# Block two's first projection: a buffer for each modulation condition, the feed-forward gate's columns moved to the mixer's output projection, one request per chunk

## The chip, the cores and the metric

The kernel runs on one core of a Trainium2 chip. The metric is the time of one execution on the device in microseconds (us). Three runs of the kernel before took 3015.27, 3014.43 and 3009.39 us, with a median of 3014.43 us. One more execution was recorded by the profiler; it took 3022.09 us, and every row below is from it.

## The reference, cut to what matters

Two transformer blocks run in sequence on 512 latent tokens of 1024 features; the second block also carries 256 context tokens. Each layer is steered by six rows of 1024 numbers (shift, scale and gate of the mixer, shift, scale and gate of the feed-forward), which come from a matrix product with a condition vector. In the second block there are two conditions, one for the latent tokens and one for the context tokens, and both see the same weights:

```python
mod = (silu_c @ ada_w[i] + ada_b[i])[:, None, :]
mod_c = (silu_cc @ ada_w[i] + ada_b[i])[None, None, :]
sh_m, sc_m, g_m, sh_f, sc_f, g_f = jnp.split(mod, 6, axis=-1)
h = modulate(rmsnorm(x, norm_mix_w[i]), sh_m, sc_m)
hc = modulate(rmsnorm(ctx, norm_mix_w[i]), shc_m, scc_m)
y, y_c = ab_mixer(h, hc, ...)              # first projection, mixing, output projection
x = x + g_m * y
x = x + g_f * swiglu(modulate(rmsnorm(x, norm_ffn_w[i]), sh_f, sc_f), w_gate, w_up, w_down)
```

The matrix `ada_w` of one layer has 1024 x 6144 numbers. The gate of the feed-forward, `g_f`, is the last of the six rows to be used: it is needed only after `w_down`.

## The kernel before, in words

Every large product is done in stages. A stage streams its weights in chunks of 128 output columns: SP loads a chunk into one of two raw buffers (`weights_raw`), ScalarE (ACT) rounds it to the high part (line L360), GpSimd (POOL) subtracts to get the low part (L406), and TensorE (PE) multiplies: two of three groups of products need the high part alone (L246, L247), the third needs the low part (L251). SP may reload a raw buffer when POOL has made the low part of what was in it. ACT, or VectorE (DVE), takes the result out of PSUM. The first two chunks of a stage that also norms or splits its input are done in another loop (L455, L456, L461), and their low parts are made by DVE (L412).

The modulation rows are computed on DVE beside such stages, as *rides*. A ride is one load of `n` blocks of 128 columns of `ada_w` into one of two buffers, then for every block and condition one multiply-and-sum of 128 x 1024 numbers (L1338), then an addition of the bias (L1343), which counts up the semaphore `added`. Ahead of the rides the conditions are loaded by SP (L1305, spread to all 128 partitions), ACT takes their sigmoid into PSUM (L1319) and DVE multiplies (L1326). A ride's load is issued by POOL (L1309 for the first two, L1313 for the others) and waits until the ride that used that buffer before has been added.

Layer 0 of block two begins with such a stage, `Project`: 12 chunks over 512 + 256 tokens, with 16 rides of two blocks, which give four of the six rows (mixer gate, feed-forward shift, scale and gate). Its instructions stand in the order that the code issues them, on each engine:
- SP: norm weights, bias, condition 0, condition 1, then the weight chunks from the third on. There is one buffer for a condition, so the load of condition 1 waits for DVE's product of condition 0, and the weight loads stand behind it.
- ACT: two high parts, 16 shifts of the norm (L1516), the sigmoids, then in turn copies out of PSUM (L2790) and high parts.
- POOL: two rides' loads, low part of chunks 2 and 3 (counted from 0); from chunk 4 to chunk 9 after each low part two loads of rides; the low parts of chunks 10 and 11 without a load; then two loads.
- DVE: norm, conditions, 16 rides, and one addition of 1 (L1351).

The next stage, `Values` (4 chunks, L2999, L3000, L3008), shares weights buffers and PSUM with it; its first product waits until `added` is at the number of rides. After the mixing itself comes the stage `GemmResidual` with the mixer's output projection: 8 chunks over all 768 tokens. There DVE splits the input (L510), makes two low parts (L412), and after each chunk adds the gated result to the residual stream (L1857); ACT squares (L1411) and POOL sums the squares (L1418) for the next norm. Other stages of this class carry rides already, between the residual additions; here there is none. The last row, `g_f`, is read first in the feed-forward's down projection, which follows.

Of the kernel before, what the change touches and what calls it, by code (L numbers as in the profile page):

```python
# [25 lines left out]
P = 128  # L26
D = 1024
KD = D // P
# [4 lines left out]
DEPTH = 2  # L33
# [1245 lines left out]
class Modulation:  # L1279
# [3 lines left out]
    def __init__(self, nc, M, ctx, s, w, b, cond, first, n, conds=2, out=None, room=None, bank=2):  # L1283
        self.nc, self.M, self.s, self.w, self.first, self.n = nc, M, s, w, first, n
        self.b, self.cond, self.conds, self.bank = b, cond, conds, bank
        self.out = M.mod_next if out is None else out
        if room:
            self.W, self.J = room
        else:
            self.W = ctx.enter_context(nc.sbuf_tensor(f"{M.blocks}_mod_w", [P, 2, n, D], F32))  # L1290
            self.J = ctx.enter_context(nc.sbuf_tensor(f"{M.blocks}_mod_c", [P, D], F32))
        self.B = ctx.enter_context(nc.sbuf_tensor(f"{M.blocks}_mod_b", [P, 2 * N_MOD], F32))
        self.acc = ctx.enter_context(nc.sbuf_tensor(f"{M.blocks}_mod_acc", [P, 2, 2 * n], F32))
        self.ready = (s["r0"], s["r1"])

    def silu_cond(self, c):
        return self.M.PS[:, self.bank + 4 * c:self.bank + 2 + 4 * c, :].rearrange("p a b -> p (a b)")

    def load(self, sp):
        s = self.s  # L1300
        sp.dma_start(self.B[:], self.b).then_inc(s["bias_in"], 16)
        for c in range(self.conds):
            if c:
                sp.wait_ge(s["summed"], c)
            sp.dma_start(self.J[:], self.cond[c].partition_broadcast(P)).then_inc(s["cond_in"], 16)  # L1305

    def load_first(self, eng):
        for u in range(2):
# [5 lines left out]

    def sigmoid(self, act):
        for c in range(self.conds):
            act.wait_ge(self.s["cond_in"], 16 * (c + 1))
            for j in range(2):
                self.nc.scalar.activation(self.M.PS[:, self.bank + 4 * c + j, :], self.J[:, j * 512:(j + 1) * 512],  # L1319
                                          ACT.Sigmoid).then_inc(self.s["sig"], 1)  # L1320

    def conditions(self, dve):
        self.nc.vector.memset(self.acc[:], 0.0).then_inc(self.s["bias_in"], 16)
        for c in range(self.conds):
            dve.wait_ge(self.s["sig"], 2 * c + 2)
            self.nc.vector.tensor_tensor(self.silu_cond(c), self.J[:], self.silu_cond(c),  # L1326
                                         ALU.mult).then_inc(self.s["summed"], 1)
        dve.wait_ge(self.s["summed"], self.conds)
        dve.wait_ge(self.s["bias_in"], 32)
# [1353 lines left out]
class Project:  # L2683
# [34 lines left out]
    def gpsimd(self, pool):  # L2718
        R, S = self.R, self.S
        if R:  # L2720
            R.load_first(pool)

            def two(pool, i, u):
                for v in range(2):
                    R.load_next(pool, 2 * i + (u - 1), v)

            pairs = (self.rides // 2 - 1) // 2
            S.lows(pool, two, pairs + 1, 1, not self.H)
            for n in range(2 * pairs + 1, self.rides // 2):
                for v in range(2):  # L2730
                    R.load_next(pool, n, v)
        else:
            S.lows(pool, first=not self.H)

# [756 lines left out]
def block_two(nc, M, A):  # L3491
# [5 lines left out]
    def tensor(ctx, name, shape, dt=F32):  # L3497
        return ctx.enter_context(M.nc.sbuf_tensor("two_" + name, shape, dt))

    with ExitStack() as ctx:  # L3500
        B = Buffers()
        B.PT, B.V = tensor(ctx, "ab_projT", [P, 12, TA]), tensor(ctx, "ab_values", [P, TA // P, 1024])
        with ExitStack() as inner:
            M.hR = tensor(inner, "ab_h_parts", [P, 2, KD, TA], F32R)
            rms_stats(nc, M, TA)
            room = (tensor(inner, "ab_mod_w", [P, 2, 2, D]), B.V[:, 2])
            ride = (modulation(A, DEPTH, 2), A["b_ada"][DEPTH], A["cond"][1], 2 * KD, 2, 2 * KD, room)
            first = Project(nc, M, inner, proj_weights(A, DEPTH), 12, B.PT, [(0, T), (T, TC)], None, ride=ride,
                            parts=(4,), KP_most=2 * KD,
                            norm=(A["norm_mix"][0], both, 0, 1, B.V[:, 0:2].rearrange("p t (u v) -> p (t u) v", v=T)))  # L3510
            run_stages(nc, [first, Values(nc, M, inner, ab_v, 1024 // VC, B.V, TA // P, ab_out, first)])
        B.mixT = tensor(ctx, "ab_mixT", [P, KD, TA])
        with ExitStack() as inner:
            B.rel = tensor(inner, "rel", [P, 8, 16 * 64])
            spatial_gate(nc, M, A, B)
            attend2(nc, M, B)
        M.hR = tensor(ctx, "ab_mix_parts", [P, 2, KD, TA], F32R)
        gemm_residual(nc, M, ab_out, M.hR, both, 2, ffn_up(A, 0, 0), mix=B.mixT, stats=True)
    feed_forward(nc, M, A, 0, both, (8, 8, 6), cd_k)

    adopt(nc, M, (1, 4))
# [249 lines left out]
```

## Time and profile before

| | |
|---|---|
| median of three runs | 3014.43 us (3009.39 to 3015.27) |
| profiled execution | 3022.09 us, of which 3020.4 us lie between its first and its last instruction |
| TensorE busy | 2652.4 us, 88% of the span; mean granted clock 0.935 |
| VectorE, ScalarE, GpSimd busy | 1465.4, 1022.3 and 788.4 us |
| first projection of block two, norm included | from 1367.9 to 1504.8 us |
| `Values` after it | from 1504.8 to 1576.9 us |
| mixer's output projection | from 1713.0 to 1795.3 us |

TensorE is busy for most of each of the three stages in the table, so the place to read is where it waits in them. A busy share of 88% says little about them. "Idle before" in a row of the timeline, in square brackets, is how long the engine had waited before that instruction, and for whom.

### The profile page before, as it was taken

What the parts mean: (1) busy time and instruction counts of PE and PEld (TensorE: products, weight loads), DVE (VectorE), ACT (ScalarE), POOL (GpSimd) and SP (SyncE); (2) the same over time, 40 slices, a digit from 0 to 9 for tenths busy, and PEclk for the clock granted to TensorE, in tenths of its full rate; (3) what the DMA queues carried; (4) which work ended last, traced back from release to release, by engine and by line L of the source; (5) the groups of instructions that cost most, each with busy time, mean ns of one, the idle gap of its engine ahead of it and who ended that gap; (6) DMA issues with size and microseconds to landing.
All of it is one profiled execution on the core that took longest, in us unless ns stands there. A gap on an engine that the chain in (4) does not pass through costs nothing. (4 is left out here: it accounts for less than half of the span.)

```text
span 3020.4 us, 41597 instructions
## 1 busy us (share of the span) xinstructions
PE 2652.4 (88%) x14918; PEld 1974.8 (65%) x14918; DVE 1465.4 (49%) x2887; ACT 1022.3 (34%) x1617; POOL 788.4 (26%) x401
## 2 busy tenths in 40 slices
PE   2998879977998869967787889999999799799997
PEld 2786453335784633326685678888888687688886
DVE  7677661335786642346706634472424575231122
ACT  3656431116566232123225632112122342322122
POOL 0451031102450311101310032232333331234443
PEclk9999889988998979988898989999999899899999
DMA  7530158953620259833611012241433311222322
GB/s 252 208 119 34 36 212 327 358 180 108 214 84 20 99 226 366 312 110 126 222 47 46 15 56 84 91 146 63 140 112 114 117 56 43 70 97 94 101 88 79
DMA packets 100697, 398.19 MB, mean 132 GB/s; under 512 B 17432, under 2 KB 27064, under 8 KB 80320
## 3 DMA queue, kind: packets, MB, share of 16 engines
q1 hardware_dynamic: 71472, 303.38, 28.7%
q0 software_dynamic: 28928, 92.30, 8.1%
q8 instruction: 90, 1.47, 0.2%
q14 instruction: 63, 0.52, 0.1%
q10 hardware_dynamic: 144, 0.52, 0.0%
HBM read 490.00 MB, written 23.59 MB: 170 GB/s over the span
## 5 line engine op out<-in xcount | busy, mean ns | idle before, releaser
L406 POOL TENSOR_TENSOR 17_w_part<-weights_raw,17_w_part 128x2048 fp32r<-128x2048 f32 (+2 forms) x44 | 146.4, 3329 | 397.2 <-ACT 17_w_part L360 397.2
L2600 DVE TENSOR_TENSOR ffn_silu<-ffn_silu,PS 128x512 f32<-128x512 f32 x66 | 37.5, 596 | 416.8 <-ACT ffn_silu L2582 416.8
L2346 PE MATMUL PS<-one_weights_more,10_h_tokens 128*64 128x512 f32 (+1 forms) x1024 | 231.2, 604 | 2.5 <-DVE 10_h_tokens L2456 2.5
L246 PE MATMUL PS<-ffn_h_parts,17_w_part 128*128 128x512 f32 (+1 forms) x640 | 202.6, 337 | 2.4 <-DVE xT L1857 1.5
L406 POOL TENSOR_TENSOR 29_w_part<-weights_raw,29_w_part 128x2048 fp32r<-128x2048 f32 (+2 forms) x36 | 147.8, 4105 | 215.1 <-ACT 29_w_part L360 215.1
L247 PE MATMUL PS<-ffn_h_parts,17_w_part 128*128 128x512 f32 (+1 forms) x640 | 201.6, 337 | 0.0
L406 POOL TENSOR_TENSOR 3_w_part<-weights_raw,3_w_part 128x1024 fp32r<-128x1024 f32 (+1 forms) x52 | 142.9, 2749 | 205.1 <-ACT 3_w_part L360 205.1
L1857 DVE SCALAR_TENSOR_TENSOR xT<-PS,mod,xT 128x512 f32 x104 | 66.3, 664 | 234.3 <-PE PS L251 201.3
L2582 ACT ACTIVATE ffn_silu<-PS 128x512 f32<-128x512 f32 x66 | 32.4, 526 | 405.7 <-PE PS L251 378.4
L2346 PEld LDWEIGHTS PS<-one_weights_more,10_h_tokens 128*64 128x64 f32 x1024 | 78.3, 139 | 133.3 <-issue 127.2
L246 PE MATMUL PS<-one_mix_parts,3_w_part 128*128 128x512 f32 x352 | 140.8, 400 | 15.2 <-ACT 3_w_part L360 15.2
L247 PE MATMUL PS<-one_mix_parts,3_w_part 128*128 128x512 f32 x352 | 139.7, 397 | 0.0
L246 PEld LDWEIGHTS PS<-ffn_h_parts,17_w_part 128*128 128x128 f32 x640 | 121.3, 190 | 15.6 <-issue 1.7
L247 PEld LDWEIGHTS PS<-ffn_h_parts,17_w_part 128*128 128x128 f32 x640 | 121.7, 190 | 13.0
L2464 DVE SCALAR_TENSOR_TENSOR 10_hid<-10_silu,one_slot_gate,PS 128x256 f32<-128x256 f32 x32 | 15.4, 480 | 233.8 <-ACT 10_silu L2427 233.8
L246 PE MATMUL PS<-ffn_h_parts,29_w_part 128*128 128x512 f32 x320 | 124.6, 389 | 0.0
L247 PE MATMUL PS<-ffn_h_parts,29_w_part 128*128 128x512 f32 x320 | 124.5, 389 | 0.0
L2369 PE MATMUL PS<-one_weights_more,10_hid_turned 128*64 128x512 f32 (+1 forms) x512 | 117.0, 598 | 2.5 <-ACT 10_hid_turned L2420 2.5
L251 PE MATMUL PS<-ffn_h_parts,17_w_part 128*128 128x512 f32 (+1 forms) x640 | 115.0, 337 | 0.0
L246 PE MATMUL PS<-ffn_hidden,17_w_part 128*128 128x512 f32 (+1 forms) x346 | 111.0, 340 | 2.6 <-ACT 17_w_part L360 2.6
L247 PE MATMUL PS<-ffn_hidden,17_w_part 128*128 128x512 f32 (+1 forms) x346 | 110.0, 340 | 0.0
L251 PEld LDWEIGHTS PS<-ffn_h_parts,17_w_part 128*128 128x128 f32 x640 | 99.8, 190 | 13.4
(666 smaller groups left out, 6591.5 us busy)
## 6 DMA issues: line engine op xcount, KB each, us to landing
one_weights_more<-in_w_gu SPq DMA_DIRECT2D x128, 1024.0 KB, 9.5
one_weights_more<-in_w_down SPq DMA_DIRECT2D x64, 1024.0 KB, 8.6
weights_raw<-in_f_gu SPq DMA_DIRECT2D x44, 1024.0 KB, 4.9
weights_raw<-in_w_proj SPq DMA_DIRECT2D x60, 512.0 KB, 3.6
one_values<-in_w_ada POOLq DMA_DIRECT2D x24, 1024.0 KB, 6.9
ffn_shared<-in_w_ada POOLq DMA_DIRECT2D x24, 1024.0 KB, 7.0
weights_raw<-in_w_ada SPq DMA_DIRECT2D x32, 512.0 KB, 9.5
two_ab_mod_w<-in_w_ada POOLq DMA_DIRECT2D x16, 1024.0 KB, 5.4
```

Of the source, the lines that this page charges most:

```text
L246: nc.tensor.matmul(out, w[0], x[1], start=(j == 0), stop=False)
L247: nc.tensor.matmul(out, w[0], x[0], start=False, stop=False)
L251: mm = nc.tensor.matmul(out, w[1], x[0], start=False, stop=(last and j == len(pairs) - 1))
L406: self.nc.gpsimd.tensor_tensor(self.part[:, u, 1], self.raw[:, u], self.part[:, u, 0].bitcast(F32), ALU.subtract).then_inc(self.count["spl ...
L1857: nc.vector.scalar_tensor_tensor(out=x, in0=M.PS[:, 4 * u + a:4 * u + a + 1, 0:nt], scalar=g, in1=x, op0=ALU.mult, op1=ALU.add).then_inc(s ...
L2346: mm = nc.tensor.matmul(M.PS[rows(h), 2 + i % 2, :], h_[:, i % 2, k, rows(h)], weights(i, h, k * 2 * FE), start=(k == 0), stop=(k == KD - 1))
L2369: mm = nc.tensor.matmul(M.PS[rows(h), 5 + part, :], hidT[:, i % 2, f, rows(h)], weights(i, h, 2 * SLOT + f * D + part * 512), start=(f == ...
L2464: nc.vector.scalar_tensor_tensor(out=hid[:, i % 2, :], in0=sl[:], scalar=D_.gate[:, u:u + 1], in1=M.PS[:, 2 + i % 2, FE:2 * FE], op0=ALU.mult,
L2582: ins = nc.scalar.activation(sl[:, u, off:off + nt], M.PS[:, 4 * u + a, 0:nt], ACT.Silu)
L2600: ins = nc.vector.tensor_tensor(sl[:, u, off:off + nt], sl[:, u, off:off + nt], M.PS[:, 4 * u + 2 + a, 0:nt], ALU.mult)
```

## The change

The diff, whole but for the header:

```diff
--- before.py
+++ after.py
@@ -1284,8 +1284,10 @@
         self.nc, self.M, self.s, self.w, self.first, self.n = nc, M, s, w, first, n
         self.b, self.cond, self.conds, self.bank = b, cond, conds, bank
         self.out = M.mod_next if out is None else out
+        self.J2 = None
         if room:
-            self.W, self.J = room
+            self.W, self.J = room[0:2]
+            self.J2 = room[2] if len(room) > 2 else None
         else:
             self.W = ctx.enter_context(nc.sbuf_tensor(f"{M.blocks}_mod_w", [P, 2, n, D], F32))
             self.J = ctx.enter_context(nc.sbuf_tensor(f"{M.blocks}_mod_c", [P, D], F32))
@@ -1296,13 +1298,16 @@
     def silu_cond(self, c):
         return self.M.PS[:, self.bank + 4 * c:self.bank + 2 + 4 * c, :].rearrange("p a b -> p (a b)")
 
+    def condition(self, c):
+        return self.J2[:] if c and self.J2 is not None else self.J[:]
+
     def load(self, sp):
         s = self.s
         sp.dma_start(self.B[:], self.b).then_inc(s["bias_in"], 16)
         for c in range(self.conds):
-            if c:
+            if c and self.J2 is None:
                 sp.wait_ge(s["summed"], c)
-            sp.dma_start(self.J[:], self.cond[c].partition_broadcast(P)).then_inc(s["cond_in"], 16)
+            sp.dma_start(self.condition(c), self.cond[c].partition_broadcast(P)).then_inc(s["cond_in"], 16)
 
     def load_first(self, eng):
         for u in range(2):
@@ -1314,16 +1319,17 @@
 
     def sigmoid(self, act):
         for c in range(self.conds):
-            act.wait_ge(self.s["cond_in"], 16 * (c + 1))
+            act.wait_ge(self.s["cond_in"], 16 * (self.conds if self.J2 is not None else c + 1))
             for j in range(2):
-                self.nc.scalar.activation(self.M.PS[:, self.bank + 4 * c + j, :], self.J[:, j * 512:(j + 1) * 512],
+                self.nc.scalar.activation(self.M.PS[:, self.bank + 4 * c + j, :],
+                                          self.condition(c)[:, j * 512:(j + 1) * 512],
                                           ACT.Sigmoid).then_inc(self.s["sig"], 1)
 
     def conditions(self, dve):
         self.nc.vector.memset(self.acc[:], 0.0).then_inc(self.s["bias_in"], 16)
         for c in range(self.conds):
             dve.wait_ge(self.s["sig"], 2 * c + 2)
-            self.nc.vector.tensor_tensor(self.silu_cond(c), self.J[:], self.silu_cond(c),
+            self.nc.vector.tensor_tensor(self.silu_cond(c), self.condition(c), self.silu_cond(c),
                                          ALU.mult).then_inc(self.s["summed"], 1)
         dve.wait_ge(self.s["summed"], self.conds)
         dve.wait_ge(self.s["bias_in"], 32)
@@ -2720,15 +2726,7 @@
         if R:
             R.load_first(pool)
 
-            def two(pool, i, u):
-                for v in range(2):
-                    R.load_next(pool, 2 * i + (u - 1), v)
-
-            pairs = (self.rides // 2 - 1) // 2
-            S.lows(pool, two, pairs + 1, 1, not self.H)
-            for n in range(2 * pairs + 1, self.rides // 2):
-                for v in range(2):
-                    R.load_next(pool, n, v)
+            S.lows(pool, R.load_next, self.rides // 2, 0, not self.H)
         else:
             S.lows(pool, first=not self.H)
 
@@ -3503,8 +3501,8 @@
         with ExitStack() as inner:
             M.hR = tensor(inner, "ab_h_parts", [P, 2, KD, TA], F32R)
             rms_stats(nc, M, TA)
-            room = (tensor(inner, "ab_mod_w", [P, 2, 2, D]), B.V[:, 2])
-            ride = (modulation(A, DEPTH, 2), A["b_ada"][DEPTH], A["cond"][1], 2 * KD, 2, 2 * KD, room)
+            room = (tensor(inner, "ab_mod_w", [P, 2, 2, D]), B.V[:, 2], B.V[:, 3])
+            ride = (modulation(A, DEPTH, 2), A["b_ada"][DEPTH], A["cond"][1], 2 * KD, 2, 3 * KD // 2, room)
             first = Project(nc, M, inner, proj_weights(A, DEPTH), 12, B.PT, [(0, T), (T, TC)], None, ride=ride,
                             parts=(4,), KP_most=2 * KD,
                             norm=(A["norm_mix"][0], both, 0, 1, B.V[:, 0:2].rearrange("p t (u v) -> p (t u) v", v=T)))
@@ -3515,7 +3513,9 @@
             spatial_gate(nc, M, A, B)
             attend2(nc, M, B)
         M.hR = tensor(ctx, "ab_mix_parts", [P, 2, KD, TA], F32R)
-        gemm_residual(nc, M, ab_out, M.hR, both, 2, ffn_up(A, 0, 0), mix=B.mixT, stats=True)
+        room = (B.V[:, 0:2].rearrange("p (u n) d -> p u n d", n=1), B.V[:, 2], B.V[:, 3])
+        gemm_residual(nc, M, ab_out, M.hR, both, 2, ffn_up(A, 0, 0), mix=B.mixT, stats=True,
+                      ride=(modulation(A, DEPTH, 1), A["b_ada"][DEPTH], A["cond"][1], 5 * KD, 1, 2, M.mod, room))
     feed_forward(nc, M, A, 0, both, (8, 8, 6), cd_k)
 
     adopt(nc, M, (1, 4))
```

The first projection has 12 rides instead of 16 (mixer gate, feed-forward shift and scale). The four others, `g_f`, become 8 rides of one block in the mixer's output projection, with their own loads of the bias and of both conditions; the buffers are pieces of the values tensor, `B.V`, which is free in both places. Each condition has a buffer of its own in both stages, ACT waits for both, and SP no longer waits for DVE between them. In the first projection POOL issues one ride's load after each low part, from the third chunk to the last.

SP at the start of the first projection, before. Semaphores show the name of their first use: `b3_conv_in` is here the count of DVE's products, `b3_summed` the count of low parts made.

```order
L1477 DMA 12_norm_w<-in_norm_mix 128x8
L1301 DMA 12_mod_b<-in_b_ada 128x96
L1305 DMA two_ab_values<-in_cond 128x1024
L1305 DMA two_ab_values<-in_cond 128x1024 [waits b3_conv_in]
L345 UNCONDITIONAL_BRANCH
L345 ISA
L349 ISA [waits b3_summed]
L349 DMA weights_raw<-in_w_proj 128x1024
```

And now:

```order
L1483 DMA 12_norm_w<-in_norm_mix 128x8
L1306 DMA 12_mod_b<-in_b_ada 128x96
L1310 DMA two_ab_values<-in_cond 128x1024 x2
L345 UNCONDITIONAL_BRANCH
L345 ISA
L349 ISA [waits b3_summed]
L349 DMA weights_raw<-in_w_proj 128x1024
```

The load of condition 1 no longer waits, and the weight loads behind it wait for low parts alone.

POOL in the first projection, before, in the loop over chunks 4 to 9 (`b3_sig` is the count of high parts, `b4_used` is `added`):

```order
L406 TENSOR_TENSOR 12_w_part<-weights_raw,12_w_part 128x1024 [waits b3_sig]
L1312 ISA
L1313 ISA [waits b4_used]
L1313 DMA two_ab_mod_w<-in_w_ada 128x2x1024
L1313 ISA [waits b4_used]
L1313 DMA two_ab_mod_w<-in_w_ada 128x2x1024
L332 REGISTER_ALU
L406 TENSOR_TENSOR 12_w_part<-weights_raw,12_w_part 128x1024 [waits b3_sig]
```

And now, in the loop over chunks 2 to 11:

```order
L406 TENSOR_TENSOR 12_w_part<-weights_raw,12_w_part 128x1024 [waits b3_sig]
L1317 REGISTER_ALU
L1318 ISA [waits b4_used]
L1318 DMA two_ab_mod_w<-in_w_ada 128x2x1024
L332 REGISTER_ALU
L406 TENSOR_TENSOR 12_w_part<-weights_raw,12_w_part 128x1024 [waits b3_sig]
```

Two loads with their waits stood between a low part and the next; now it is one.

DVE in the mixer's output projection, before, from the split of the input to the first residual addition (`b3_cond_in` is the count of finished chunks):

```order
L510 TENSOR_TENSOR two_ab_mix_parts<-two_ab_mixT,two_ab_mix_parts 128x768 [waits b3_added] x8
L412 TENSOR_TENSOR 16_w_part<-weights_raw,16_w_part 128x1024 [waits b3_sig] x2
L1849 UNCONDITIONAL_BRANCH
L1849 ISA
L1857 ISA [waits b3_cond_in]
L1857 REGISTER_ALU
L1857 SCALAR_TENSOR_TENSOR xT<-PS,mod,xT 128x512
L1857 ISA
L1857 SCALAR_TENSOR_TENSOR xT<-PS,mod,xT 128x256
```

And now, from the two low parts to the bias of the first ride; the residual addition, L1863, comes behind it (`b3_affine` is the count of sigmoids, `b3_taken` the landing of a ride's load):

```order
L412 TENSOR_TENSOR 16_w_part<-weights_raw,16_w_part 128x1024 [waits b3_sig] x2
L1329 MEMSET 16_mod_acc 128x4
L1332 TENSOR_TENSOR PS<-two_ab_values,PS 128x1024 [waits b3_affine] x2
L1855 UNCONDITIONAL_BRANCH [waits b3_iw_done,b3_conv_in]
L1855 ISA
L1344 ISA two_ab_values,16_mod_acc<-two_ab_values,PS 128x1024 [waits b3_taken]
L1344 ISA 16_mod_acc 128x1
L1347 ISA
L1344 ISA two_ab_values,16_mod_acc<-two_ab_values,PS 128x1024 [waits b3_conv_in]
L1344 ISA 16_mod_acc 128x1
L1347 REGISTER_ALU
L1349 ISA [waits b3_conv_in]
```

The conditions' products and a ride of two sums now stand ahead of each residual addition.

## Rows read from the trace of the kernel before

**Rows 1.** Windows: window, length, busy time (count) by engine, granted clock, DMA, GB/s.
```profile
core 0: us, PE busy (x) PEld busy (x) DVE busy (x) ACT busy (x) POOL busy (x), PEclk, DMA share, GB/s
1401.00:1405.00 4.00, 3.69 (x9) 2.92 (x10) 3.83 (x8) 2.08 (x4) 3.65 (x2) 0.50 0.03 10
1412.00:1454.00 42.00, 42.00 (x242) 37.10 (x241) 27.90 (x50) 9.88 (x16) 14.71 (x11) 1.00 0.59 201
1505.00:1510.00 5.00, 5.00 (x24) 5.00 (x25) 0.00 (x0) 1.67 (x1) 3.26 (x1) 0.50 0.01 3
```
**Rows 2.** Timeline of TensorE: start, duration, engine, line, operation, [idle before <- releaser].
```profile
1401.32 0.79 PE L246 MATMUL PS<-two_ab_h_parts,12_w_part 128*128 128x512 f32 x1 [8.04 <-ACT 12_w_part L360]
1411.53 0.40 PE L246 MATMUL PS<-two_ab_h_parts,12_w_part 128*128 128x512 f32 x1
...
1444.97 0.40 PE L246 MATMUL PS<-two_ab_h_parts,12_w_part 128*128 128x512 f32 x1
...
1471.85 4.23 PE L251 MATMUL PS<-two_ab_h_parts,12_w_part 128*128 128x512 f32 x16 [2.79 <-POOL 12_w_part L406]
1475.88 0.63 PE L246 MATMUL PS<-two_ab_h_parts,12_w_part 128*128 128x512 f32 x1
...
1504.84 0.56 PE L2999 MATMUL PS<-12_w_part,two_ab_h_parts 128*128 128x256 f32 x1 [10.12 <-DVE mod L1351]
```
**Rows 3.** Waits in projection and `Values`: who waited for whom: total us, times, longest.
```profile
POOL two_ab_mod_w L1313 <- DVE mod L1343: 43.6, 12, 4.7
...
PE PS L251 <- POOL 12_w_part L406: 5.4, 3, 2.8
```
**Rows 4.** Timeline of SP's queue in the first projection.
```profile
1392.92 0.33 SPq L1305 DMA_DIRECT2D two_ab_values<-in_cond  x1
1393.64 78.75 SPq L349 DMA_DIRECT2D weights_raw<-in_w_proj  x10
```
**Rows 5.** Timeline of ScalarE in the first projection.
```profile
1389.22 1.28 ACT L1319 ACT_TABLE_LOAD   x1
...
1397.27 1.12 ACT L1319 ACTIVATE PS<-two_ab_values 128x512 f32<-128x512 f32 x2 [5.64 <-DMA two_ab_values<-in_cond]
1398.33 0.85 ACT L2790 ACTIVATE two_ab_projT<-PS 128x512 f32<-128x512 f32 x2
1400.21 1.06 ACT L360 ACTIVATE 12_w_part<-weights_raw 128x1024 fp32r<-128x1024 f32 x1 [1.03 <-DMA weights_raw<-in_w_proj]
...
1477.39 1.06 ACT L360 ACTIVATE 12_w_part<-weights_raw 128x1024 fp32r<-128x1024 f32 x1 [0.31 <-ACT two_ab_projT L2790]
```
**Rows 6.** Timeline of GpSimd in the first projection.
```profile
1468.69 0.72 POOL L1313 DMA_DIRECT2D two_ab_mod_w<-in_w_ada  x1 [4.54 <-DVE mod L1343]
1469.43 2.37 POOL L406 TENSOR_TENSOR 12_w_part<-weights_raw,12_w_part 128x1024 fp32r<-128x1024 f32 x1
...
1485.93 0.74 POOL L1313 DMA_DIRECT2D two_ab_mod_w<-in_w_ada  x1 [0.33 <-DVE mod L1343]
```
**Rows 7.** Timeline of VectorE at the end of the first projection.
```profile
1493.96 1.22 DVE L1338 CUSTOM_DVE_ANT_0 two_ab_values<-two_ab_mod_w,PS 128x1024 f32<-128x1024 f32 x1 [3.05 <-DMA two_ab_mod_w<-in_w_ada]
...
1499.24 1.22 DVE L1338 CUSTOM_DVE_ANT_0 two_ab_values<-two_ab_mod_w,PS 128x1024 f32<-128x1024 f32 x1
...
1504.43 0.16 DVE L1343 TENSOR_TENSOR mod<-12_mod_acc,12_mod_b 128x4 f32 x1 [0.18 <-DVE 12_mod_acc L1338]
```
**Rows 8.** Tile `two_ab_mod_w` (1 MB a load): issue to landing of its loads.
```profile
DMA to landing us min/median/max: 5.2/5.4/9.4
```
**Rows 9.** Timeline of VectorE in the mixer's output projection.
```profile
1722.77 2.35 DVE L412 TENSOR_TENSOR 16_w_part<-weights_raw,16_w_part 128x1024 fp32r<-128x1024 f32 x2
1735.77 2.19 DVE L1857 SCALAR_TENSOR_TENSOR xT<-PS,mod,xT 128x512 f32 x4 [10.65 <-PE PS L461]
...
1787.65 1.14 DVE L1857 SCALAR_TENSOR_TENSOR xT<-PS,mod,xT 128x512 f32 x2 [7.23 <-PE PS L251]
```
**Rows 10.** Tile `7_mod_w`, block one's rides of one block (0.5 MB): issue to landing.
```profile
DMA to landing us min/median/max: 3.5/5.0/6.3
```

## The prediction, made before the changed kernel had run

> **What bounds the kernel now.** I read the timeline of TensorE first, for its gaps, then the queues of the engines it waited for, then the windows for the clock. In steady state the first projection of block two is bound by TensorE: chunk 3 starts at 1411.53 and chunk 7 at 1444.97, four chunks in 33.44 us, 8.36 us each, with TensorE busy for all of the 42.00 us of that window at full clock, 2.4 GHz [rows 1, 2]. Everything else in the stage is a wait of TensorE, and there are three kinds.
>
> The first is the gap of 8.04 us before chunk 2 [rows 2]. The releaser named is ACT's high part, but that one waited for weights [rows 5], and SP's queue shows why: the load of condition 1 left at 1392.92, and the first of ten weight loads behind it at 1393.64 [rows 4]. The second is the three waits for a low part, 5.4 us together [rows 3]: the longest, 2.79 us at 1471.85 [rows 2], ends with a low part that POOL could begin at 1469.43 only, because it had waited 4.54 us for DVE to free a ride's buffer [rows 6]. POOL waited so 12 times, 43.6 us in all [rows 3]. The third is the gap of 10.12 us before `Values` [rows 2], until DVE has finished the last ride [rows 7]. DVE is not late by its own work alone: the last but one ride waited 3.05 us for a load [rows 7] that POOL had issued behind two low parts [rows 6].
>
> After each long gap the granted clock is 0.50, the level of 1.2 GHz: in 1401 to 1405 and in 1505 to 1510 [rows 1].
>
> **The change part by part.** All sums go against the profiled execution, 3022.09 us (span 3020.4).
>
> *A buffer for each condition.* SP's weight loads are no longer behind DVE's product. They wait for low parts that DVE makes during the first pair of chunks, so they land well before that pair ends at 1393.28 (1401.32 less 8.04). Both conditions land early too: the one issued at 1392.92 let ACT start at 1397.27, 4.35 us later [rows 4, 5], and ACT first asks for them at 1389.22. From there ACT needs 1.28 for the table and twice 1.12 for four sigmoids [rows 5], to 1392.7, so it is free when the pair ends. Then come a copy (0.85), a hand-over of about 0.31, and the high part (1.06) [rows 5]: chunk 2 starts 2.2 us after the pair, at 1395.5. The gap goes from 8.04 to 2.2: **5.8 us**. Chunk 2 itself took 10.21 us (1401.32 to 1411.53) against 8.36, as its first part ran at the lower clock; if the short gap keeps the clock, that is **1.85 us**. For the shorter gap the bounds are the waits in this stage: behind the one of 2.79 us, 16 products took 4.23 us and the next matmul 0.63 us, where the same kind takes 0.40 in the steady state [rows 2]; so it may not be kept, and I hold 0 to 1.85, taking 1.85 because 2.2 is below 2.79.
>
> *One request per chunk, 12 rides.* Chunks 3 to 11 took from 1411.53 to 1494.72 (1504.84 less 10.12), 83.19 us; nine chunks of 8.36 are 75.24. The excess, **7.95 us**, is the three waits and what the clock lost behind them. Would a low part still be late? POOL's order is now low part, wait, load. Rides begin about 1394.4, behind the sigmoids and DVE's two products, and take 5.35 us each (1499.24 to 1504.59, [rows 7]); the load after low part n needs ride n-2 to be done. That holds POOL only for the first two or three chunks, until about 1411, when low parts have over 5 us before TensorE asks for them (high products take two thirds of 8.36). Later a chunk of 8.36 is longer than a ride of 5.35, so POOL does not wait. I take all 7.95, with 5 as the low bound.
>
> *The end of the rides.* With chunk 2 at 1395.5, chunk 10 starts at 1462.4 and chunk 11 ends at 1479.1. The last load follows low part 11. ACT makes high part 11 at 1.51 us into chunk 10 (1477.39 against 1475.88, [rows 2, 5]), done at 2.6; the low part of 2.37 [rows 6] is done at 5.0. The load lands 5.2 to 9.4 us later, median 5.4 [rows 8], and the one that shared the DMA engines with the weights of `Values` took 8.0 (1485.93 to 1493.96, [rows 6, 7]). That sharing is there again, since SP's load waits for the same low part. With 5.4 the last ride ends 15.8 us after chunk 10's start, with 8.0 it ends at 18.4; chunk 11 ends at 16.7. So TensorE waits 0 to 1.9 us (0.25 from DVE's end to its start included); I take 1.0. The gap of 10.12 becomes 1.0: **9.1 us**. The Trainium skill (DMA: Bandwidth & Descriptors, Anatomy of one DMA — SWDGE (gpsimd) path) puts such a transfer at 2.0 us plus its bytes over 436 GB/s, which would be, as an estimate, 4.4 us and no wait at all, a gain of 28.2 in place of 27.2 below. The trace does not agree: its shortest is 5.2.
>
> *The start of `Values`.* The five microseconds from 1505 ran at half the clock [rows 1]; without the long gap that returns half of them, **2.5 us**.
>
> *The rides in the mixer's output projection.* What moves there: on SP a bias and two conditions ahead of the weight loads, which start over 10 us later; on POOL two loads at the start and six between low parts and sums, at most 0.74 each [rows 6]; on ACT a table load and four sigmoids (3.5 us) behind the split, inside a wait that lasts to the end of the first pair; on DVE two products (1.23 each, as an estimate the same as a sum's 1.22) and 8 rides of two sums, 2.8 us each (half of 5.35 and the bias). DVE stands idle 10.65 us before the first residual addition and 7.23 before the last [rows 9]: 2.5 + 2.8 fit in the first, 2.8 in the second. A ride stands ahead of a residual addition, so a late load would hold it. A low part ends about 3.7 us into a chunk (1.06 and 2.37 with hand-overs), and the load is out at 4.5; it lands 3.5 to 6.3 us later [rows 10], the ride takes 2.8, and the residual addition is due at the end of the chunk's successor but one. There is room for a landing of 17 us, except in the last chunk, where the addition is on the path to the norm: there the limit is 9.4 us (load out 4.5 us into the chunk that starts two times 8.36 before the residual addition at 1787.65 [rows 9], so at 1775.4). **0 us**, between -0.5 and 3.
>
> Sum: 5.8 + 1.85 + 7.95 + 9.1 + 2.5 = 27.2 us, so 2994.9 us for an execution like the profiled one. That one stood 7.7 us above the median of the runs, 3014.43, from which I take the 27.2: **2987 us**.
>
> **The rivals.**
> 1. The rides still set the end. If the last load takes the longest landing, 9.4 us [rows 8], the last ride ends 19.8 us after chunk 10's start and the gap is 3.3, long enough for the lower clock, as the one of 2.79 shows. The gain loses 2.3 and 2.5: 22.4 us, 2992 us. For it speaks that two 1 MB transfers go out together; against it that the worst comparable one took 8.0.
> 2. The change does not do what it says: the gap before chunk 2 stays, because the weights or the second condition land late for another reason. It gives back 5.8 + 1.85: gain 19.6, 2995 us. Against it: 21 us lie between the stage's start at 1367.9 and the first use of a condition at 1389.22 [rows 5].
> 3. The work is moved, not hidden. If nothing of DVE's work in the output projection were covered, it would cost 8 x 2.8 + 2.5, some 25 us, and the kernel would stay within 0.2% (3012 us). Against it are the idle times in [rows 9].
> 4. Slower than before: loads of the rides in the output projection land late, DVE holds the residual additions, and PSUM banks come free late. It costs TensorE time from a landing of 17 us on, twice over the eight chunks, and the norm from 9.4 us on; to eat 27.2 us all of them need about 24 us, and then 3018 us or more. The longest in [rows 10] is 6.3.
>
> **How the numbers follow.** My forecast has 0.80, rival 1 0.07, rival 2 0.04, rival 3 0.05, rival 4 0.04. The forecast's own range is a gain of 20 to 30 us (the clock in the short gap, 3 us of waits left, 1.9 at the end, 3 in the output projection; above, no wait at the end and the rest of a colder start); with the spread of the runs, 3009 to 3015, I give 2978 to 3001 us, which holds rivals 1 and 2. A measurement of this kernel can tell about 0.2%, 6 us, from no change. Faster by more than that: forecast, rivals 1 and 2, 0.91; within it: rival 3, 0.05; slower: rival 4, 0.04.
>
> **What would show it.** In the new profile SP's second condition leaves right behind the first and the weights follow before 1390; TensorE's gap before chunk 2 is 2 to 3 us, chunk 2 takes 8.4; no wait for a low part above 0.5 us; the gap before `Values` is under 2 us, and the stage with the norm lasts some 112 us instead of 137. The output projection keeps its 82 us. I am wrong if DVE or POOL appears as TensorE's releaser in the output projection, or if the gap before `Values` is 4 us or more.

## The result, and the profile after

The changed kernel took 2985.02 us (median of four runs, 2981.76 to 2988.96), the kernel before 3014.85 us (four runs, 3009.39 to 3017.19). The ratio is 0.9903 with a 95% interval of 0.9890 to 0.9917: 29.8 us less, the interval is 25 to 33. The forecast was 2987 us, a gain of 27.2 in a range of 20 to 30.

The two profiled executions, 3022.09 and 2985.17 us, lie 36.9 us apart, more than the medians. The stages show where. From the first product of the projection to the first product of the feed-forward, all that the change touches, before took 429.4 us and after 400.2: 29.2 us. Another 6.6 us lie ahead of it, in code that did not change: the first product comes at 1372.4 in the profile of before and at 1365.8 after, and over the profiles of all the kernels below between 1361.2 and 1372.4. The remaining 1.1 us lie behind. So the profiled execution of before was a late one, and all that follows is measured from the first product of the projection on.

TensorE in the changed kernel, at the starts of chunk 2 and of `Values` (start, duration, engine, line, operation, idle before and releaser):

```profile
1388.14 0.50 PE L246 MATMUL PS<-two_ab_h_parts,12_w_part 128*128 128x512 f32 x1 [1.51 <-ACT 12_w_part L360]
1388.48 0.39 PE L247 MATMUL PS<-two_ab_h_parts,12_w_part 128*128 128x512 f32 x1
...
1455.14 0.40 PE L246 MATMUL PS<-two_ab_h_parts,12_w_part 128*128 128x512 f32 x1
...
1473.34 0.36 PE L2997 MATMUL PS<-12_w_part,two_ab_h_parts 128*128 128x256 f32 x1 [1.32 <-DVE mod L1357]
1473.54 0.28 PE L2998 MATMUL PS<-12_w_part,two_ab_h_parts 128*128 128x256 f32 x1
```

These answer to [rows 2]. The gap of 8.04 us is one of 1.51, the gap of 10.12 one of 1.32, and the first products behind them take 0.50 and 0.36 us, where those of before took 0.79 and 0.56; the second ones take 0.39 and 0.28, as in the steady state. Chunk 2 starts at 1388.14 and chunk 10 at 1455.14: eight chunks in 67.00 us, 8.375 each, all at the pace of the steady state. The windows behind the two gaps show the clock (window, length, busy time by engine, granted clock, DMA share, GB/s):

```profile
1388.00:1392.00 4.00, 3.86 (x17) 3.19 (x18) 3.90 (x7) 1.91 (x4) 2.41 (x1) 1.00 0.11 10
1473.00:1478.00 5.00, 4.66 (x39) 4.69 (x40) 0.26 (x2) 1.91 (x1) 2.75 (x1) 1.00 0.49 197
```

1.00, the level of 2.4 GHz, in both; [rows 1] had 0.50. Who waited for whom from 1365 to 1560:

```profile
POOL two_ab_mod_w L1318 <- DVE mod L1349: 8.9, 4, 3.2
...
PE PS L246 <- ACT 12_w_part L360: 1.5, 1, 1.5
...
PE PS L2997 <- DVE mod L1357: 1.3, 1, 1.3
```

TensorE's waits for a low part are gone from the list, and POOL's for a ride's buffer went from 43.6 us in 12 times [rows 3] to 8.9 in four. The queues show the two causes. SP, then ACT ahead of chunk 2:

```profile
1362.36 0.90 SPq L1310 DMA_DIRECT2D two_ab_values<-in_cond  x2
1375.98 68.33 SPq L349 DMA_DIRECT2D weights_raw<-in_w_proj  x10
```
```profile
1382.62 1.28 ACT L1324 ACT_TABLE_LOAD   x1
1383.92 2.16 ACT L1324 ACTIVATE PS<-two_ab_values 128x512 f32<-128x512 f32 x4
1386.01 0.85 ACT L2788 ACTIVATE two_ab_projT<-PS 128x512 f32<-128x512 f32 x2
1387.03 1.06 ACT L360 ACTIVATE 12_w_part<-weights_raw 128x1024 fp32r<-128x1024 f32 x1 [0.17 <-ACT two_ab_projT L2788]
```

Both conditions leave together, the weights 13.6 us later, 11 us before ACT asks for them; the four sigmoids run without a break, where those of the second condition had stood 5.64 us [rows 5]. And the end of the rides, on POOL and on DVE:

```profile
1457.77 2.39 POOL L406 TENSOR_TENSOR 12_w_part<-weights_raw,12_w_part 128x1024 fp32r<-128x1024 f32 x1 [5.33 <-ACT 12_w_part L360]
1460.11 0.74 POOL L1318 DMA_DIRECT2D two_ab_mod_w<-in_w_ada  x1
```
```profile
1467.72 1.22 DVE L1344 CUSTOM_DVE_ANT_0 two_ab_values<-two_ab_mod_w,PS 128x1024 f32<-128x1024 f32 x1 [2.60 <-DMA two_ab_mod_w<-in_w_ada]
...
1472.92 0.16 DVE L1349 TENSOR_TENSOR mod<-12_mod_acc,12_mod_b 128x4 f32 x1 [0.18 <-DVE 12_mod_acc L1344]
1473.13 0.17 DVE L1357 TENSOR_SCALAR mod<-mod 128x16 f32<-128x16 f32 x1
```

The last load goes out at 1460.11 and lands 7.6 us later, when the sum starts; the last ride ends 17.9 us after chunk 10's start. All twelve loads of this tile, issue to landing, and then the seven that leave from 1410.96 on:

```profile
DMA to landing us min/median/max: 5.3/6.7/10.8
```
```profile
DMA to landing us min/median/max: 6.3/6.8/8.3
```

The median is later than before [rows 8]. Each of the seven leaves within 0.5 us of a load of weights. The three ahead of them leave 1.8 us or more behind one and land after 5.3 to 5.5 us; the first two, which leave beside the two conditions, after 8.8 and 10.8.

### The profile page after: what moved, and what is told of

It is laid out like the page before. It is cut to its first block and busy times, and to the rows that moved or that the text cites. A ratio compares the mean times of both kernels' runs of the same rounds, so it can differ in the third digit from the quotient of the medians.

```text
span 2983.5 us, 41616 instructions
## 1 busy us (share of the span) xinstructions
PE 2640.4 (88%) x14918; PEld 1964.7 (66%) x14918; DVE 1480.1 (50%) x2894; ACT 1025.2 (34%) x1622; POOL 790.8 (27%) x405
## 5 line engine op out<-in xcount | busy, mean ns | idle before, releaser
L1863 DVE SCALAR_TENSOR_TENSOR xT<-PS,mod,xT 128x512 f32 x104 | 66.4, 664 | 196.7 <-PE PS L251 169.3
L246 PEld LDWEIGHTS PS<-ffn_h_parts,17_w_part 128*128 128x128 f32 x640 | 121.3, 190 | 15.6 <-issue 1.7
L247 PEld LDWEIGHTS PS<-ffn_h_parts,17_w_part 128*128 128x128 f32 x640 | 121.5, 190 | 13.1
L2375 PE MATMUL PS<-one_weights_more,10_hid_turned 128*64 128x512 f32 (+1 forms) x512 | 117.0, 598 | 2.6 <-ACT 10_hid_turned L2426 2.6
L360 ACT ACTIVATE 17_w_part<-weights_raw 128x2048 fp32r<-128x2048 f32 (+2 forms) x46 | 65.7, 1432 | 125.3 <-PE PS L251 117.7
```

Source lines behind the costliest of these rows:

```text
L246: nc.tensor.matmul(out, w[0], x[1], start=(j == 0), stop=False)
L247: nc.tensor.matmul(out, w[0], x[0], start=False, stop=False)
L360: self.nc.scalar.activation(self.part[:, u, 0], self.raw[:, u], ACT.Copy).then_inc(self.count["high_done"], 1)
L1863: nc.vector.scalar_tensor_tensor(out=x, in0=M.PS[:, 4 * u + a:4 * u + a + 1, 0:nt], scalar=g, in1=x, op0=ALU.mult, op1=ALU.add).then_inc(s ...
L2375: mm = nc.tensor.matmul(M.PS[rows(h), 5 + part, :], hidT[:, i % 2, f, rows(h)], weights(i, h, 2 * SLOT + f * D + part * 512), start=(f == ...
```

## The experiments

Diffs are against the changed kernel and cut to the lines that matter, with `...` for arguments left out; the comments that begin with # are mine. A first set takes the change apart. Three edits undo one part each:

```diff
# the old order: two requests per low part from the second pair on, the rest at the end
-            S.lows(pool, R.load_next, self.rides // 2, 0, not self.H)
+            def two(pool, i, u):
+                for v in range(2):
+                    R.load_next(pool, 2 * i + (u - 1), v)
+            pairs = (self.rides // 2 - 1) // 2
+            S.lows(pool, two, pairs + 1, 1, not self.H)
+            for n in range(2 * pairs + 1, self.rides // 2):
+                for v in range(2):
+                    R.load_next(pool, n, v)
# one buffer for the conditions
-            room = (tensor(inner, "ab_mod_w", [P, 2, 2, D]), B.V[:, 2], B.V[:, 3])
+            room = (tensor(inner, "ab_mod_w", [P, 2, 2, D]), B.V[:, 2])
# all 16 rides in the projection, none in the output projection
-            ride = (..., 2 * KD, 2, 3 * KD // 2, room)
+            ride = (..., 2 * KD, 2, 2 * KD, room)
-        gemm_residual(nc, M, ab_out, M.hR, both, 2, ffn_up(A, 0, 0), mix=B.mixT, stats=True, ride=(...))
+        gemm_residual(nc, M, ab_out, M.hR, both, 2, ffn_up(A, 0, 0), mix=B.mixT, stats=True)
```

The table has the total with its ratio to before, and from the profiles the stretches: from the first product to chunk 2 (A), chunk 2 to the start of the projection's last product (B), from there to the first product of `Values` (C: the gap and that product's own 0.28 us), from there to the start of the last product of `Values` (D), and the whole from the first product of the projection to the first of the feed-forward (E), in us.

| kernel | total (runs), us | ratio, 95% interval | A | B | C | D | E |
|---|---|---|---|---|---|---|---|
| before | 3014.85 (4) | | 28.9 | 93.1 | 10.4 | 71.7 | 429.4 |
| buffers alone | 3009.37 (12) | 0.9988 (0.9974 to 1.0003) | 22.4 | 91.1 | 10.3 | 71.1 | 420.3 |
| columns moved alone | 3004.01 (6) | 0.9962 (0.9949 to 0.9974) | 27.9 | 87.4 | 7.1 | 70.5 | 417.4 |
| moved and buffers | 2996.43 (5) | 0.9939 (0.9926 to 0.9952) | 22.4 | 85.0 | 6.9 | 71.1 | 410.7 |
| moved and order | 2995.68 (6) | 0.9936 (0.9924 to 0.9948) | 27.8 | 86.1 | 1.6 | 69.1 | 407.2 |
| the whole change | 2985.02 (4) | 0.9903 (0.9890 to 0.9917) | 22.4 | 83.6 | 1.6 | 69.1 | 400.2 |

The four parts were compared with 17 runs of before on their chip, 3013.19 us in the median. E is from one profile each.

**Buffers alone** (old order, 16 rides, none moved).

> The buffers alone: two condition buffers, but 16 rides in the first projection, the old order of requests on GpSimd, and no rides in the output projection. My theory: the gap before chunk 2 falls from 8.04 to about 1.5 us and chunk 2 runs at full clock (8.4 us instead of 10.2), while the three waits for low parts (5.4 us) and the gap before Values (10.1 us) stay, since rides and chunks move up together: gain 7 to 9 us. Rival (the conditions' order does not matter, the whole gain is that of the rides): gain under 2 us, gap still 8 us.

The gap before chunk 2 goes, the late low parts and the gap before `Values` stay. TensorE's waits, 1360 to 1520, and the start of `Values` with the clock behind it:

```profile
PE PS L3005 <- DVE mod L1357: 10.1, 1, 10.1
...
PE PS L251 <- POOL 12_w_part L406: 5.3, 3, 2.7
PE PS L246 <- ACT 12_w_part L360: 1.5, 1, 1.5
```
```profile
1487.91 0.55 PE L3005 MATMUL PS<-12_w_part,two_ab_h_parts 128*128 128x256 f32 x1 [10.07 <-DVE mod L1357]
```
```profile
1485.00:1492.00 7.00, 4.09 (x19) 4.12 (x20) 2.59 (x6) 1.91 (x1) 2.21 (x1) 0.50 0.01 2
```

In its stages it gains 9.1 us; the totals show 3.8 (3013.19 less 3009.37), and the interval reaches from a gain of 7.8 to a loss of 0.9. That difference stays open: the runs of this kernel scatter from 3000.50 to 3013.88 us, those of before on that chip from 3001.47 to 3019.96.

**Columns moved alone** (12 rides, old order, one buffer).

> The gate's columns moved alone: 12 rides in the first projection, 8 small ones in the output projection, but one condition buffer in the first projection and GpSimd's old order. My theory: the gap of 8.0 us before chunk 2 stays, the waits for low parts go (about 8 us with what the clock lost), and the gap before Values stays at some 6 to 8 us, because the last two loads are issued one behind the other after the last low part: gain 9 to 13 us. Rival (four rides fewer are enough for the end): gap before Values under 2 us, gain 18 to 20 us.

```profile
PE PS L246 <- ACT 12_w_part L360: 7.0, 1, 7.0
PE PS L3005 <- DVE mod L1357: 6.8, 1, 6.8
...
PE PS L251 <- POOL 12_w_part L406: 1.0, 1, 1.0
```

Four rides fewer take two of the three waits for a low part with them, but of the gap before `Values` only 3.3 us. The last two loads stand behind all low parts on POOL, so DVE is idle for 16.2 us until the first of them has landed, and then has two rides to do where the whole change has one. E falls by 12.0 us.

**Moved and buffers** (all but the new order).

> The whole change without the new order: two condition buffers, 12 rides, but GpSimd issues two requests per chunk from chunk 4 to 7 and the last two behind all low parts. My theory: gap before chunk 2 about 1.5 us, no waits for low parts, gap before Values 6 to 8 us with the lower clock behind it, so 7 to 10 us slower than the changed kernel, gain 17 to 22 us. Rival (the order is worth nothing, the number of rides decides): gap before Values under 2 us, gain as with the whole change, 27 to 30 us.

```profile
PE PS L3005 <- DVE mod L1357: 6.7, 1, 6.7
...
PE PS L251 <- POOL 12_w_part L406: 1.1, 1, 1.1
```

A falls to 22.4 as with the buffers alone, C stays at 6.9. One late low part is left, where I had expected none. What the order is worth is the difference to the whole change: 10.5 us of E, of which 5.3 in C, 2.1 in D and 1.4 in B; the rest lies behind `Values`. The totals show a gain of 16.8 us (3013.19 less 2996.43), a little under the 17 to 22 that I had expected.

**Moved and order** (all but the second buffer).

> The whole change without the second condition buffer in the first projection. My theory: the gap of 8.0 us and the slow chunk 2 are back, all else as in the changed kernel, with a gap before Values of 1 to 2 us: 7 to 9 us slower than the changed kernel, gain 19 to 22 us. Rival (with only 12 rides the late start of the weights is made up for later): within 2 us of the changed kernel.

```profile
PE PS L246 <- ACT 12_w_part L360: 6.9, 1, 6.9
...
PE PS L2997 <- DVE mod L1357: 1.3, 1, 1.3
```

No wait for a low part is left and C is 1.6, while the gap before chunk 2 stays at 6.9. The buffer is thus worth 7.1 us of E on top of the rest: 5.4 in A and 2.5 in B, where chunk 2 starts at the lower clock, less 0.9 elsewhere. In the totals this kernel gains 17.5 us, under the 19 to 22 that I had expected, while its E falls by 22.2; its profiled execution, 2987.50 us, was its fastest. The gap before chunk 2 comes from the single buffer alone. For the gap before `Values` fewer rides are not enough without the order; the order with all 16 rides was not tried.

A second set asks about the parts that the forecast had put at nothing or at a bound.

**No rides in the output projection.** The gate's columns are computed nowhere, so this kernel leaves out part of the computation:

```diff
-        gemm_residual(nc, M, ab_out, M.hR, both, 2, ffn_up(A, 0, 0), mix=B.mixT, stats=True, ride=(...))
+        gemm_residual(nc, M, ab_out, M.hR, both, 2, ffn_up(A, 0, 0), mix=B.mixT, stats=True)
```

> The changed kernel with the 8 rides of the output projection left out, so the columns of the feed-forward gate are not computed at all. My theory (they lie wholly beside TensorE's work): from the first product of the output projection to the first of the feed-forward 84 us as with them (84.2), total within 2 us of the changed kernel's. Rival (the moved rides cost something there): that stretch shorter by 1 us or more.

2990.88 us against 3017.13 of before (17 runs, as for the rest of this set), ratio 0.9916 (0.9903 to 0.9930): no faster than the whole change. The median is 5.9 us above that of the whole change, where I had expected 2; the intervals of the ratios overlap, and E is 400.6 us against 400.2. From the first product of the output projection to the first of the feed-forward it takes 84.1 us, the whole change 84.2, before 84.9. No cost of the rides there shows: 0.2 us is the difference of two single executions.

**Last loads ahead of the low parts.**

```diff
-            S.lows(pool, R.load_next, self.rides // 2, 0, not self.H)
+            S.wait(pool, "split_done", 2)
+            with pool.Fori(1, S.pairs - 1) as i:
+                for u in range(2):
+                    S.low(pool, 2 * i + u, u)
+                    R.load_next(pool, i, u)
+            for u in range(2):
+                R.load_next(pool, S.pairs - 1, u)
+                S.low(pool, 2 * S.pairs - 2 + u, u)
```

> The changed kernel, but for the last two chunks of the first projection GpSimd issues the ride's load ahead of the low part. My theory (what is left of the gap before Values, 1.3 us, is the landing of the last load, issued behind the last low part): that gap falls to about 0.2 us, no wait for a low part above 0.5 us, the stretch from the first projection to the feed-forward 1 us shorter; in the total within the noise. Rival (the last load is late because it shares the DMA engines with the weights of Values): gap still over 1 us.

POOL, then DVE, at the end of the projection:

```profile
1458.14 0.74 POOL L1318 DMA_DIRECT2D two_ab_mod_w<-in_w_ada  x1 [4.05 <-DVE mod L1349]
1460.11 2.40 POOL L406 TENSOR_TENSOR 12_w_part<-weights_raw,12_w_part 128x1024 fp32r<-128x1024 f32 x1 [1.23 <-ACT 12_w_part L360]
```
```profile
1468.80 0.18 DVE L1357 TENSOR_SCALAR mod<-mod 128x16 f32<-128x16 f32 x1
```

And TensorE's last low products of chunk 11:

```profile
1471.41 2.84 PE L251 MATMUL PS<-two_ab_h_parts,12_w_part 128*128 128x512 f32 x15
```

The landing of that last load, and when the weights of `Values` that stand behind low part 11 leave on SP:

```profile
DMA to landing us min/median/max: 5.2/5.2/5.2
```
```profile
1462.68 0.33 SPq L349 DMA_DIRECT2D weights_raw<-in_ab_v  x1
```

The rides are done at 1468.97, before TensorE is. C falls from 1.6 to 0.1 us, so nothing is left of the gap of 1.32, and E to 397.9. That the last ride was what ended the 1.32 us is shown. Which of the two theories is right is not shown, as the edit takes both causes away. The load leaves 0.7 us after chunk 10's start (1457.48) where it left 5.0 us after it. It also lands in 5.2 us where it took 7.6, now that it leaves 4.5 us ahead of those weights. By these numbers either alone, 4.3 or 2.4 us, would have covered the 1.32. In the total, 2984.46 us and a ratio of 0.9902 (0.9887 to 0.9917), it can't be told from the whole change.

**Every sum two and four times over in the output projection** (the same numbers are written again).

```diff
-        K = C * self.n
+        K = C * self.n * self.repeat        # 2 or 4 in the output projection, 1 elsewhere
-        for j in range(K):
+        for jj in range(K):
+            j = jj // self.repeat
```

> The changed kernel with every multiply-and-sum of the output projection's rides done twice (same result). Theory A (VectorE's idle time there covers them, and also as much again): VectorE has 5.2 us of sums, the bias and 1.14 us of residual additions in 8.36 us of a chunk; TensorE does not wait, the stage stays at 84 to 85 us. Theory B (the bias addition takes 2 us beside GpSimd's work, which leaves 8.6 us a chunk): TensorE begins to wait, 1 to 5 us more.

> The same with every sum four times. Both theories: 10.2 us of sums, 1.1 of residual additions and 0.5 to 2.3 for the bias are longer than a chunk of 8.36 us, so the residual additions hold the PSUM banks and the stage follows VectorE: 8 times 11.8 to 13.6 us, 30 to 48 us more than the changed kernel, so slower than the kernel before. It shows the price of the rival in which VectorE holds the residual additions.

Twice: 2987.37 us, ratio 0.9913 (0.9897 to 0.9930); the output projection with the norm takes 0.9 us more than in the whole change. DVE at its end, with the last ride's first sum and the last residual addition:

```profile
1749.28 1.22 DVE L1344 CUSTOM_DVE_ANT_0 two_ab_values<-two_ab_values,PS 128x1024 f32<-128x1024 f32 x1 [1.07 <-DMA two_ab_values<-in_w_ada]
...
1754.81 1.14 DVE L1865 SCALAR_TENSOR_TENSOR xT<-PS,mod,xT 128x512 f32 x2 [0.17 <-issue]
```

The load for that ride left at 1740.88 and took 8.4 us, and the ride of four sums then held the addition to 1754.81, 1.17 us after TensorE's last product; in the whole change it comes 0.26 us after. This is the 0.9 us. Theory A had the stage at 84 to 85 us, theory B 1 to 5 us more; it is 85.1, and the wait behind it is that for the norm's squares, 2.7 us where it was 1.8.

Four times: 3015.88 us against 3017.13, ratio 1.0000 (0.9990 to 1.0009), with 32.8 us more there, 117.0 in place of 84.2. I had expected it slower than before; it gives the gain back and no more. DVE with four times the sums, two residual additions and what stands ahead of them, and TensorE's waits, 1690 to 1830:

```profile
1741.97 0.16 DVE L1349 TENSOR_TENSOR mod<-16_mod_acc,16_mod_b 128x2 f32 x1 [0.18 <-DVE 16_mod_acc L1344]
1742.30 1.14 DVE L1865 SCALAR_TENSOR_TENSOR xT<-PS,mod,xT 128x512 f32 x2 [0.17 <-issue]
...
1753.60 0.16 DVE L1349 TENSOR_TENSOR mod<-16_mod_acc,16_mod_b 128x2 f32 x1 [0.18 <-DVE 16_mod_acc L1344]
1753.93 1.14 DVE L1865 SCALAR_TENSOR_TENSOR xT<-PS,mod,xT 128x512 f32 x2 [0.17 <-issue]
```
```profile
PE PS L246 <- DVE xT L1865: 12.2, 6, 3.8
PE PS L1430 <- ACT 16_stat_sq L1417: 8.7, 1, 8.7
...
PE PS L1430 <- POOL inverse_roots L1424: 5.8, 1, 5.8
```

From one residual addition to the next DVE needs 11.63 us and is never idle for more than 0.2, a chunk of TensorE takes 8.36: TensorE waits for PSUM six times and then for the norm's statistics, which stand behind the last additions. The granted clock falls with it, to 0.88 from 1708 to 1775, where the changed kernel has 1.00 from 1701 to 1751.5. With twice the sums DVE needs 6.6 to 8.35 us from one addition to the next, as the addition of the bias takes up to 2.2 of them; that is still within a chunk, and TensorE's wait for the residual additions stays at 0.5 us. This is the mechanism of rival 4, brought about by longer rides: for PSUM with four times the sums, for the norm already with twice and one load of 8.4 us.

## Why the prediction was right

All five terms came out within 1 us. Against the stretches of the table:

| step of the prediction | forecast, us | measured, us | from |
|---|---|---|---|
| gap before chunk 2 | 5.8 | 6.5 | 8.04 to 1.51 |
| chunk 2 and chunks 3 to 11 | 1.85 + 7.95 = 9.8 | 9.5 | B, 93.1 to 83.6 |
| gap before `Values` | 9.1 | 8.8 | 10.12 to 1.32 |
| start of `Values` | 2.5 | 2.7 | D, 71.72 to 69.07 |
| output projection with the norm | 0 | 0.7 | 84.9 to 84.2 |

The sum is 28.2; the other 1.0 us of the 29.2 lie between `Values` and the output projection. No change was made in that stretch, but it took 140.3 to 141.4 us in the four profiles with a gap of 6.7 us or more before `Values`, and 138.9 to 139.9 in the six with a shorter one or none; why was not followed up. The 0.7 of the last row is not the rides' doing either: the stretch takes 83.8 to 84.2 us in the other profiles that do each sum at most once, with rides there or without. So 1.7 of the 2.0 us above the forecast come from nothing that its working named.

*A buffer for each condition.* The mechanism is as told: without the second buffer and with all the rest, the gap stays at 6.9 us. The gap left over is 1.51 and not 2.2: the pair ends at 1386.63 (1388.14 less 1.51), and the copy that I had put behind that end starts 0.62 us ahead of it, at 1386.01, as soon as the sigmoids are done: it takes out chunk 0, whose products end before the pair does. The clock in the short gap, which I held open between 0 and 1.85 us, was kept: a gap of 1.51 left the clock at 2.4 GHz, one of 2.79 did not [rows 2]. Whether the 2.2 of the working would have kept it, no run shows; here the 1.85 us owe something to luck. Rival 2, another cause for that gap, falls with the gap.

*One request per chunk, 12 rides.* That no low part would be late is borne out: the wait is gone from the list, and B is ten chunks of 8.36. POOL waited for rides four times, until 1410.96, where the working had two or three chunks, until about 1411. The working named the order of POOL as the cause; the parts show that the number of rides does most of it: with both buffers B falls by 6.2 us with fewer rides and by 1.4 more with the order. Fewer rides without the order leave one wait, of 1.0 us with one buffer and 1.1 with two; the order, given fewer rides, takes the last one.

*The end of the rides.* The last ride was forecast 15.8 to 18.4 us after chunk 10's start, by a landing of 5.4 to 8.0; it came at 17.9, by 7.6. So the landing under load is the right row to take, and the median of [rows 8] is not: in the changed kernel the median itself is 6.7. TensorE waited 1.32 us, forecast 1.0, between 0 and 1.9. The estimate of 4.4 us, by the Trainium skill (DMA: Bandwidth & Descriptors, Anatomy of one DMA — SWDGE (gpsimd) path), is missed again: the shortest landing is 5.3. Rival 1, with a gap of 3.3 us, needed a landing of 9.4; the longest beside a load of weights was 8.3, and the 10.8 is a load at the stage's start, beside the conditions.

*The rides in the output projection.* No cost of theirs shows: 84.2 us with them, 84.1 without. Rival 3 would have been 25 us. The working was incomplete in two places. It had DVE's ride at 2.8 us, and it takes up to 5.4 there (1700.96 to 1706.33), since the bias addition stretches (below); that is hidden because the chunk leaves 8.36 us and the residual addition needs 1.14. And it took 6.3 us [rows 10] as the longest landing, where the last load here took 7.5 (issued at 1738.41), under the limit of 9.4. One sign of being wrong, DVE as TensorE's releaser in the output projection, did appear, with the 0.5 us that it had before the change too, so it told nothing.

The forecast took its gain off the median of the runs, 3014.43, although the profiled execution stood at 3022.09. That was sound as far as the profiles tell: of the 36.9 us between the two profiled executions 6.6 lie ahead of the projection, in code that did not change.

## What to carry to other kernels

Work moved beside a stage bound by TensorE was nearly free here as long as DVE's time per chunk, with its own part, stayed within the chunk's: up to 8.35 of 8.36 us cost 0.9, and that in the last chunk, where the addition is on the path to the norm; 11.6 cost 32.8. Work off the critical path can still set it through the queue that it stands in: here one shared buffer held the weight loads behind DVE's product, and two requests per low part held the low parts behind DVE's rides; the queue order on SP and POOL told of both, and the share of busy time of neither. To price a load that has to land in time, take landings that had to share the DMA engines, not the median.

## What the runs showed of the hardware

DVE's bias addition (L1349, 128 x 2 numbers, both inputs in SBUF) takes 0.16 us alone, and up to 2.71 in the output projection. DVE, then POOL, in the changed kernel:

```profile
1703.62 2.71 DVE L1349 TENSOR_TENSOR mod<-16_mod_acc,16_mod_b 128x2 f32 x1 [0.18 <-DVE 16_mod_acc L1344]
...
1717.05 0.16 DVE L1349 TENSOR_TENSOR mod<-16_mod_acc,16_mod_b 128x2 f32 x1 [0.18 <-DVE 16_mod_acc L1344]
...
1722.08 2.08 DVE L1349 TENSOR_TENSOR mod<-16_mod_acc,16_mod_b 128x2 f32 x1 [0.18 <-DVE 16_mod_acc L1344]
```
```profile
1703.89 2.41 POOL L406 TENSOR_TENSOR 16_w_part<-weights_raw,16_w_part 128x1024 fp32r<-128x1024 f32 x1
...
1714.31 1.86 POOL L1424 TENSOR_TENSOR inverse_roots<-16_stat_sq 128x768 f32<-128x768 f32 x1
...
1722.28 1.86 POOL L1424 TENSOR_TENSOR inverse_roots<-inverse_roots,16_stat_sq 128x768 f32<-128x768 f32 x1
```

The long ones end at 1706.33 and 1724.16, POOL's operations at 1706.30 and 1724.14: the addition lasts until POOL's operation on two inputs is done, five times of eight, for 2.00 to 2.71 us. The short one at 1717.05 falls where POOL stands idle, from 1716.17 on. The sums of 128 x 1024 take 1.22 us beside the same POOL operations; one of their inputs is in PSUM.

This agrees with the Trainium skill (SBUF — State Buffer, SBUF: two separate sides), by which DVE and GpSimd share a pair of ports that one of them holds for a whole instruction, so that a DVE operation with two inputs in SBUF waits while GpSimd reads there. That the one that starts first gets the ports, as the same section says, does not show: both long additions above start before POOL's operation, by 0.27 and 0.20 us, while POOL still issues a load, and lose. Whether the issue of the load held the ports was not tried, and a page of the profile calls the spans on POOL rough.

It held the residual additions behind the first two long ones, which start as soon as the bias is added, at 1706.25 and 1713.34. Behind the other three the residual addition waits 2.5 us more for TensorE, as this one behind the bias of 1722.08:

```profile
1726.72 1.15 DVE L1863 SCALAR_TENSOR_TENSOR xT<-PS,mod,xT 128x512 f32 x2 [2.55 <-PE PS L251]
```

TensorE it held by nothing: its one wait for them is 0.5 us, as before.
